# SSD's sums of squares in a two-layer encoder kernel: squares as the moving operand in four groups of 32 array columns, added up on VectorE

## What is computed

```
proj = h @ w_in
z, xbc, dt_f, dt_b, q_mem = split(proj)
xbc = silu(depthwise_conv_centred(xbc, conv_w, conv_b))
xs, bm, cm = split(xbc)
y = (y_fwd + y_bwd + d_skip[:, None] * xs).reshape(b, t, BRANCH_WIDTH)
y = rmsnorm(y * silu(z[..., :BRANCH_WIDTH]), norm_g)
mixed = concatenate([y, m])
x = x + rmsnorm(mixed @ w_out[0], post_g[0])
```

## Time and profile before

| | |
|---|---|
| runs of the kernel before | 2177.12, 2178.52, 2180.94 us (median 2178.52) |
| the profiled execution | 2177.56 us, of which its span is 2175.8 us |
| TensorE busy | 2117.3 us (97% of the span) |
| VectorE busy | 1088.1 us (50% of the span; 545 us of the 650 between 430 and 1080) |
| ScalarE, GpSimd busy | 729.5 us, 933.6 us |
| records of L1797 (squares) | 192, from 453.0 to 1001.8 us |

### The profile page before, as it was taken

The page is one execution under the profiler, slowest core; times in us unless marked ns, Lnnn a source line. Parts: engine busy times, 40 slices in busy tenths (PEclk is TensorE's granted clock), DMA queues, the critical chain, the costliest instruction groups (busy, mean ns, idle before and its releaser), DMA issues.

```text
span 2175.8 us, 31436 instructions
## 1 busy us (share of the span) xinstructions
PE 2117.3 (97%) x12922; PEld 1809.6 (83%) x12922; DVE 1088.1 (50%) x1686; ACT 729.5 (34%) x1686; POOL 933.6 (43%) x623
## 2 busy tenths in 40 slices
PE   7999999999999999999999999999999999999997
PEld 6888887788888888887788887888888888888885
DVE  4103332688888887898721323125324433451447
ACT  4123122344353353443332212034423333432354
POOL 4533333242433443333753332655454445454544
PEclk9999999999999999999999999999999999999999
DMA  5221112343323232234441111231132213122213
GB/s 194 88 70 52 50 57 74 125 106 98 104 78 97 88 107 73 74 117 145 156 136 49 58 49 49 85 105 57 50 89 72 59 58 90 54 58 83 79 50 116
DMA packets 206810, 184.72 MB, mean 85 GB/s; under 512 B 23915, under 2 KB 172683, under 8 KB 206667
## 3 DMA queue, kind: packets, MB, share of 16 engines
q1 hardware_dynamic: 206667, 182.72, 27.4%
HBM read 168.71 MB, written 12.21 MB: 83 GB/s over the span
## 4 chain that ended last, share of the span: by engine, by line
PE 49%; DVE 4%; issue 1%; ACT 0%; DMA 0%; POOL 0%; DVEq 0%; POOLq 0%
PE bank L214 24%; PE bank L264 9%; PE bank L567 6%; PE bank L2281 2%; PE bank L2309 2%; PE bank L1000 2%; PE bank L2292 2%; PE bank L1026 1%; DVE acc L911 1%; PE bank L1064 1%; DVE acc L915 1%; DVE acc L905 0%; PE bank L440 0%; PE bank L2353 0%; DMA R<-macc_dram 0%
## 5 line engine op out<-in xcount | busy, mean ns | idle before, releaser
L188 POOL TENSOR_SCALAR Wh<-Wraw 128x1024 fp32r<-128x1024 f32 x217 | 254.5, 1173 | 1123.8 <-issue 754.5
L214 PE MATMUL bank<-Hh,Wh 128*128 128x512 f32 (+1 forms) x1936 | 664.1, 343 | 6.4 <-ACT R L1201 3.6
L214 PE MATMUL bank<-Hl,Wh 128*128 128x512 f32 (+1 forms) x1936 | 651.4, 336 | 0.0
L214 PE MATMUL bank<-Hh,Wl 128*128 128x512 f32 (+1 forms) x1936 | 650.5, 336 | 0.0
L191 POOL TENSOR_TENSOR Wl<-Wraw,Wh 128x1024 fp32r<-128x1024 f32 x217 | 550.8, 2538 | 18.1
L214 PEld LDWEIGHTS bank<-Hh,Wh 128*128 128x128 f32 x1936 | 367.1, 190 | 54.7 <-issue 14.2
L214 PEld LDWEIGHTS bank<-Hh,Wl 128*128 128x128 f32 x1936 | 366.7, 189 | 39.0
L214 PEld LDWEIGHTS bank<-Hl,Wh 128*128 128x128 f32 x1936 | 367.3, 190 | 36.5 <-issue 1.7
L298 DVE TENSOR_TENSOR acc<-bank,acc 128x512 f32<-128x512 f32 x240 | 164.9, 691 | 168.8 <-PE bank L264 167.8
L264 PE MATMUL bank<-Wh,Mh 128*128 128x512 f32 x528 | 208.7, 395 | 11.4 <-DVE acc L298 11.3
L264 PE MATMUL bank<-Wh,Ml 128*128 128x512 f32 x528 | 205.7, 390 | 0.0
(11 more groups left out here) (246 smaller groups left out, 3067.5 us busy)
## 6 DMA issues: line engine op xcount, KB each, us to landing
Wraw<-in_na_w_in_dram SPq DMA_DIRECT2D x80, 512.0 KB, 3.7
Wraw<-in_ssd_w_in_dram SPq DMA_DIRECT2D x57, 512.0 KB, 4.2
Wraw<-in_w_out_dram SPq DMA_DIRECT2D x48, 512.0 KB, 3.3
R<-acs_dram SPq DMA_DIRECT2D x16, 1536.0 KB, 6.2
Wraw<-in_w_mem_kv_dram SPq DMA_DIRECT2D x32, 512.0 KB, 3.8
R<-gs_dram SPq DMA_DIRECT2D x32, 128.0 KB, 3.5
R<-R SPq DMA_DIRECT2D x32, 128.0 KB, 3.6
macc_dram<-acc SPq DMA_DIRECT2D x1, 3072.0 KB, 9.1
```

Of the source, the lines that this page charges most:

```text
L188: pool.tensor_scalar(Wh[:, s, :], Wraw[:, s, :], 1.0, 1.0, ALU.mult, ALU.mult).then_inc(pool_c, 1)
L214: mm = pe.matmul(DB[h.k % 2][:, 0:t1 - t0], w[:, k, :], x[:, k, t0:t1], start=(k == 0 and i == 0), stop=(k == KC - 1 and i == 2))
```

## The change

The operands of squares change places. The ones are now the stationary operand, 32 columns of them, and z moves, in four pieces of 192 tokens. Piece q goes to the array columns 32q to 32q + 31 and so to the partitions 32q to 32q + 31 of A[0], columns 256 to 447, every one of the 32 partitions with the same sums. There is one such area for all steps. So VectorE adds it after each step to a buffer "rows" in SBUF (add_rows; the first time a copy), between its second decay product and the carried states of the step that follows. Squares wait until the rows before are added (rows_added), and so does y, which writes to the same bank.

After the 16th step rows holds all sums with the tokens along the columns. TensorE turns them back (turn_sums: three transposes and a matmul with the identity), in the work behind the loop, and four small copies take the place of the reduction. Semaphores of layer 0 that nothing uses are no longer made, and some buffers move.

```diff
-        NR, TAIL = 25032, 1352
+        NR, TAIL = 25032, 1280
...
-                self.cw, self.dcol, self.ssum, self.sd = r(160), r(PAIRS), r(NT), r(NT)
+                self.rows, self.ssum, self.sd, self.dcol, self.cw = r(192), r(NT), r(NT), r(PAIRS), r(160)
...
+                def add_rows(n, signal, value):
+                    dve.wait_ge(signal, value)
+                    new = A[0][:, 256:256 + ROW]
+                    if n:
+                        i = dve.tensor_tensor(rows, new, rows, ALU.add)
+                    else:
+                        i = dve.tensor_copy(rows, new)
+                    i.then_inc(rows_added, 1)
...
                     dve.tensor_tensor(seg, seg, both_heads(cb_l), ALU.mult).then_inc(dec_ready, 1)

+                    if n:
+                        add_rows(n - 1, sq_summed, n)
                     dve.wait_ge(prev_set, n + 1)
...
                         dve_out_tiles(dve, half, (2 * k, 2 * k + 1))
-                        dve.wait_ge(summed, 1)
+                        if half == k == 0:
+                            add_rows(LAST, summed, 1)
                         nxt.mem_norm.dve_low(dve, 2 * half + k)
...
                     if half == 0:
-                        dve.tensor_reduce(ssum, A[0][:, 256:256 + PAIRS * NT].rearrange("p (n i) -> p i n", i=NT), AXX,
-                                          ALU.add).then_inc(reduced, 1)
+                        dve.wait_ge(sums_turned, 1)
+                        turned = A[0][:, 0:384].rearrange("p (b q r) -> p b q r", b=3, r=64)
+                        by_three = ssum.rearrange("p (q i) -> p i q", i=3)
+                        for p0, p1, i, b, r in ((0, P, 0, 0, 0), (0, P, 2, 1, 32), (0, 64, 1, 2, 0), (64, P, 1, 2, 32)):
+                            m = dve.tensor_copy(by_three[p0:p1, i, :], turned[p0:p1, b, :, r])
+                            if r != 32 or p0 == 0:
+                                c.add(m)
+                        m.then_inc(reduced, 1)
...
                 def squares(n, signal=sq_summed):
                     pe.wait_ge(sq_done, n + 1)
-                    for i in range(NT):
-                        mm = pe.matmul(A[0][:, 256 + n * NT + i:257 + n * NT + i], z[:, i * P:(i + 1) * P],
-                                       ones[:, 0:1], start=True, stop=True)
+                    if n:
+                        pe.wait_ge(rows_added, n)
+                    for q in range(4):
+                        mm = pe.matmul(A[0][32 * q:32 * q + 32, 256:256 + ROW], ones[:, 0:32],
+                                       z[:, q * ROW:(q + 1) * ROW], start=True, stop=True)
                     mm.then_inc(signal, 1)
+
+                def turn_sums():
+                    pe.wait_ge(rows_added, PAIRS)
+                    pe.wait_ge(gated, PAIRS)
+                    pe.transpose(A[0][:, 0:P], rows[:, 0:P], ident[:, :])
+                    pe.transpose(A[0][:, P:2 * P], rows[:, 64:ROW], ident[:, :])
+                    pe.transpose(A[0][0:64, 256:256 + P], rows[:, P:ROW], ident[:, :])
+                    pe.matmul(A[0][64:P, 256:256 + P], rows[:, 0:64], ident[:, :], start=True, stop=True)\
+                        .then_inc(sums_turned, 1)
...
                     if n:
                         pe.wait_ge(gated, n)
+                        pe.wait_ge(rows_added, n)
                     pe.wait_ge(carried, n + 1)
...
                         nxt.mem_norm.pe(pe, 2 * half + k)
+                    if half == 0:
+                        turn_sums()
                     pe_out_tiles(pe, (4, 5), last_mix)
```

More of the change, by code:

```diff
@@ L621, in memory_phase @@
             post_gain_landed, summed, added, post_sums, post_root, post_scaled, x1_stored = (
-                sem(n + x) for x in ("post_gain_landed", "summed", "added", "post_sums", "post_root", "post_scaled",
-                                     "x1_stored"))
-            macc_landed, res_landed = ([sem(f"{n}{x}{i}") for i in range(2)] for x in ("macc_landed", "res_landed"))
+                sem(n + x) if L else None for x in ("post_gain_landed", "summed", "added", "post_sums", "post_root",
+                                                    "post_scaled", "x1_stored"))
+            macc_landed, res_landed = ([sem(f"{n}{x}{i}") for i in range(2)] if L else None
+                                       for x in ("macc_landed", "res_landed"))
             where = InOrder() if L == 0 else ByColumn()
@@ L1411, in ssd_phase @@
             LAST = PAIRS - 1
+            ROW = 192
+            rows = pre.rows
+            rows_added, sums_turned = sem("g_rows_added"), sem("g_sums_turned")
             def group_unit(n):
```

## The result

The changed kernel is slower. Median 2189.84 us in 9 runs (2182.20 to 2195.34), the kernel before 2178.63 in 9 runs of the same session (2176.00 to 2180.94): ratio 1.0051, 95% interval 1.0037 to 1.0065, or 11.2 us. The prediction said 2181.9, in a range of 2176 to 2189. Its forecast (rival A, up to two more falls of the clock) did not come; its rival B (slower, more falls) did, and two things beside it that it had not priced. For the four falls that the profile shows, B alone had 2185.1.

The account below looks back on a forecast made before the run. TensorE and VectorE were taken to lead the SSD stage in turn. To the median of 2178.5 us came +0.1 for the steps, +0.1 for the stage's end and +3.2 for two clock falls: 2181.9 us, range 2176 to 2189.

Parts of the forecast that it names:

- rival A: SSD stage: VectorE takes TensorE's gain, up to two more clock falls, 2178.7 to 2182 us; chance 0.44.
- rival B: SSD stage: clock falls behind three or more of eight waits; three +5.0 us, six 2188.3; chance 0.36.
- Squares: TensorE, each step: four array groups overlap, 0.56 us against 1.26, so 0.70 us less a step.
- in pairs: Squares on TensorE if only two array groups overlap: 0.16 us less gain, 0.54 a step.
- Add: VectorE, steps 1 to 15: one new 128x192 add from PSUM, 0.27 us, waiting for nothing.
- The path sum: Shifts carried through TensorE and VectorE hand-overs, steps 1 to 15: nine later, six earlier, together +0.1 us.
- Waits in steps 1, 5, 9: TensorE's waits there grow by 0.97 us, to 2.1 or 2.2 us.
- Step 14: TensorE's wait of 2.8 us there grows to 3.8 us; the step ends 0.27 us later.
- Steps 4, 8 and 12: TensorE's waits grow to 2.1 to 2.4 us; each step ends later by the add, 0.27 us.
- Rival D: Waits are not VectorE's own; its work between hand-overs shrinks, up to -11.2 us, 2167.3; chance 0.12.
- The clock: Half clock behind TensorE's longer waits in the stage: two more falls of 1.6 us each, +3.2 us.
- The end of the stage: Last add hidden, turn of the sums 0.75 us on TensorE, costing 0 to 0.4 us, taken as 0.1.

Follow-up runs that it names:

- the hold alone: Changed kernel, GpSimd's fourth splitting unit in steps 4, 8, 12 waiting for VectorE's second decay product, no useless matmuls; 2186.16 us against 2176.98 before.
- the kernel held in the norm: Changed kernel, GpSimd's sixth weight unit in layer 1 waiting until the first norm tile is scaled and added; 2185.72 us against 2176.67 before.
- with fillers: Kernel before the change, with useless fp32 matmuls sized for TensorE's own waits in the stage; 2176.58 us against 2178.03 without.

## Why the prediction was wrong

Three terms of the sum failed: the clock (two more falls taken, four in the profile), the length of VectorE's other instructions (held constant; 0.85 us more in each of three steps), and everything behind the stage (taken at nothing, without a reason; 6.8 us in the norm of layer 1). The other terms follow in the order of the prediction.

**Squares: right.** 0.70 us saved a step, as the sum took it. The block itself is 0.10 shorter than worked out and the states ahead of it 0.10 longer, and the two cancel, which is luck. The side case "in pairs" is added up wrongly: four slots of 0.16 us and 0.23 make 0.87, a gain of 0.39 and not 0.54. Nothing hangs on it.

**Add: right.** Pitch 0.26 to 0.27 us, no wait; +0.25 in step 4 with the hold, where nothing else disturbs.

**The path sum: too high.** For steps 1 to 13 it has -0.4 us, and -2.1 is measured. In the profile of the hold alone, without the steps that half clock touches, the steps change as follows (from the start of turning x to the start of turning the next):

| steps | forecast each | measured each |
|---|---|---|
| 4, 8, 12 | +0.27 | +0.25 to +0.29 |
| 5, 13 | +0.27 | -0.05, +0.06 |
| 2, 6, 10 | -0.31 | -0.19, -0.38, -0.38 |
| 3 | -0.70 | -0.70 |
| 7, 11 | -0.33 | -0.70 |

Steps 1 and 9 changed by +0.05 and +0.06 in the changed kernel, where +0.27 each was forecast. So VectorE took less back than I charged. In step 7 I let the add use up VectorE's only visible wait of 0.60, and it did not reach the path; which of VectorE's work gave way I did not look into. This alone would have made a slightly faster kernel.

**Waits in steps 1, 5, 9: right** (2.0, 1.9, 1.9; forecast 2.1 to 2.2). **Step 15: right** (2.6; forecast 2.5). **Step 14: 3.2, forecast 3.8. Steps 4, 8 and 12: here a term failed**, 2.9 to 3.0 us against 2.1 to 2.4. I shifted VectorE by its own new instruction and left the duration of the others as they were. Rival D spoke of VectorE's work changing when GpSimd's splitting moves, but only as a gain. It was this mechanism with the other sign: 3 x 0.85 us.

**The clock: the mechanism right, the number wrong.** "I take two more falls in the run" is the term that failed: the profile has four new ones in the stage, the norm's beside. A fall's price stood: steps 1, 9 and 14 of the hold alone, each with one, are 1.45, 1.57 and 1.67 us longer, where I took 1.6. What I did not see is that the length of a wait decides little. The prediction says that the clock fell once in the kernel before. The same profile has a second fall, the longer of the two: 6.8 us from 1003.8, which begins 0.6 us before a wait of only 1.40 us ends. TensorE's wait, then one stretch (us, busy time and count of PE, granted clock, DMA share, GB/s):

```profile
1004.43 0.77 PE L264 MATMUL bank<-Wh,S14h 128*128 128x512 f32 x1 [1.40 <-DVE acc L298]
```

```profile
1004.00:1010.00 6.00, 5.57 (x14) 0.50 0.28 83
```

This row, which the prediction does not weigh, speaks against a length from which waits count. In the changed kernel four waits of 2.9 to 3.2 us were followed by half clock; in the kernel held in the norm the waits of 2.90, 3.00 and 2.90 us in steps 4, 8 and 12 were not, and two of 1.86 and 1.87 in steps 5 and 9 were (630.8, 787.9). With eight waits near 2 us or longer, two falls was a guess towards the low end, and B, at 0.36, should have had more than A.

The stage can be added up now: steps 1 to 13 without disturbance -2.1, product +2.5, four falls +6.4, and -3.1 for the kernel before's own stretch at 1003.8 (6.2 of its 6.8 us lie behind the wait), which is absent here: +3.7, against 4.0 measured. That absence is luck, and the forecast had not counted on it.

**The end of the stage: right in size** (the turn takes 0.78 us from 1016.79, forecast 0.75; what it costs the path is not isolated).

**The norm: not in the prediction**, which closes its sum with the end of the stage. It is the largest piece of the profiled execution. I looked for who is late next in the stage and stopped at its end, though VectorE carries the shift on into products that share time with GpSimd. What puts the fifth unit's weights so late is open: SyncE issues that transfer behind one that waits for VectorE, which fits, but no run isolates it.

## What to carry over

An instruction taken from the leading engine, where it then waits for another, buys idle time, and here idle time was worse than the work: 0.7 us of useless matmuls a step made the changed kernel 7.8 us faster, by less half clock and by collisions that did not happen. Before such an edit, list every wait that grows and charge a fall of the clock to most of those that come near a length behind which one has been seen, the shortest such length too. And follow the engine that ends late into the stage behind. And wherever VectorE reads two operands from SBUF beside GpSimd, ask who starts first: a shift of 0.7 us turned a lead of 0.42 into a lag of 0.27 and cost 0.85 us each time.

## What the runs showed of the hardware

- Four array groups of 32 columns, moving 192 fp32 columns each, run side by side: 8 records in 0.46 us to the next dense one; the dense block ahead of them takes 0.10 us more.
- A VectorE product of two SBUF operands (128x1536) takes 1.75 us, and 2.60 when GpSimd's 1.26-us instruction started 0.27 us ahead of it; one of 128x1024 takes 1.23 us, and up to 3.43 beside a split. When VectorE starts first, GpSimd's instruction stretches instead (1.05 to 2.24 us).
- The granted clock fell to half behind or during waits of TensorE of 1.78 to 4.9 us and, in two profiles of the kernel before (plain, and with fillers), during one of 1.40; mostly for 3.4 us, sometimes 6.8. It stayed at full behind others of up to 3.0. In three profiles it fell at 272 us with no wait, behind 3 to 4 us of matmuls with 32 and 64 moving columns.
- Runs of the changed kernel with a mean clock of 0.990 took 2194.4 and 2195.3 us, the one with 0.996 took 2182.2. The eight runs with GpSimd held alone split in the same way: 0.995 in the three under 2180.1, 0.992 to 0.994 in the five from 2186.1 up.
